# One transformer-block kernel: search bits in one set, per-unit score waits, and flags, sine arguments and new rows in pieces

## What is computed

```python
def _dsa_sparse_attention(q, k, v, q_idx, k_idx, w_idx):
    ...
        logits = jnp.einsum('bqhd,bsd->bqhs', qib, k_idx).astype(jnp.float32)
        score = jnp.einsum('bqhs,bqh->bqs', jax.nn.relu(logits), wb)
        limit = (tp // CHUNK + 1) * CHUNK
        admissible = key_pos[None, :] < limit[:, None]
        score = jnp.where(admissible[None], score, -jnp.inf)
        _, sel = lax.top_k(score, topk)
    ...
def _hybrid_layer(x, mem, cos, sin, ...):
    h = _rmsnorm(x, g_in)
    proj = h @ w_in
    ...
    y_a = _sliding_window_sink_attention(a_q, a_k, a_v, attn_sinks)
    y_b = _dsa_sparse_attention(b_q, b_k, b_v, b_qi, b_ki, b_wi)
    y_c = _memory_cross_attention(c_q, m_k, m_v)
    ys = jnp.stack([y_a * jax.nn.silu(a_z), y_b * jax.nn.silu(b_z), y_c * jax.nn.silu(c_z)], axis=2)
    u = jnp.einsum('bsnc,ncd->bsnd', ys, w_branch)
    merged = jnp.sum(jax.nn.sigmoid(gates) * u, axis=2)
    return x + merged @ w_out
```

## Time and profile before

| | |
|---|---|
| median of 3 runs | 3076.94 us (3074.46 to 3077.45) |
| the profiled execution | 3070.94 us, span 3069.2 us |
| busy: TensorE, VectorE, ScalarE, GpSimd | 2618.7, 1831.2, 1340.2, 474.3 us |
| mean granted TensorE clock | 0.931 of full speed |

### The profile page before, as it was taken

The page is one execution under the profiler, slowest core; times in us unless marked ns, Lnnn a source line. Parts: engine busy times, 40 slices in busy tenths (PEclk is TensorE's granted clock), DMA queues, the critical chain, the costliest instruction groups (busy, mean ns, idle before and its releaser), DMA issues.

```text
span 3069.2 us, 36940 instructions
## 1 busy us (share of the span) xinstructions
PE 2618.7 (85%) x13093; PEld 2163.2 (70%) x13093; DVE 1831.2 (60%) x3925; ACT 1340.2 (44%) x2550; POOL 474.3 (15%) x367
## 2 busy tenths in 40 slices
PE   4797988989888999998878898889888788877996
PEld 4575876867777778776667677777666566766785
DVE  3367665442677777315777767731588796666622
ACT  3354543332655444214656434431475672433511
POOL 3424243442010010101010010010101001000010
PEclk8898999989999999998989999999998889989998
DMA  3546564675443421454242421145424224001044
GB/s 120 196 159 201 163 213 144 214 258 186 151 148 105 145 98 63 169 198 155 92 142 97 130 90 42 42 164 196 155 86 134 83 96 137 28 21 34 30 165 158
DMA packets 172343, 399.33 MB, mean 130 GB/s; under 512 B 13568, under 2 KB 96512, under 8 KB 162176
## 3 DMA queue, kind: packets, MB, share of 16 engines
q1 hardware_dynamic: 172160, 396.96, 39.2%
HBM read 308.31 MB, written 88.60 MB: 129 GB/s over the span
## 4 chain that ended last, share of the span: by engine, by line
PE 46%; DVE 21%; ACT 14%; issue 12%; POOL 3%; DMA 3%; SPq 1%; DVEq 0%; ACTq 0%; POOLq 0%
PE PJ L760 31%; PE TR L661 5%; PE PV L727 5%; ACT signs L923 4%; DVE above L1353 2%; ACT ptH L912 2%; DVE ptL L1272 2%; ACT prob L899 2%; DVE prob L1233 2%; ACT prob L889 2%; DVE nmx L1243 2%; PE SC L670 1%; PE SC L671 1%; ACT squared L868 1%; DVE flags L1420 1%
## 5 line engine op out<-in xcount | busy, mean ns | idle before, releaser
L760 PE MATMUL PJ<-hH,pairs 128*128 128x512 f32 (+1 forms) x3584 | 1174.7, 398 | 56.9 <-POOL pairs L1055 18.3
L760 PEld LDWEIGHTS PJ<-hH,pairs 128*128 128x128 f32 x3584 | 690.1, 194 | 206.9 <-issue 37.6
L760 PE MATMUL PJ<-hL,pairs 128*128 128x512 f32 (+2 forms) x1792 | 711.8, 397 | 0.0
L923 ACT ACTIVATE signs<-score,bits 128x384 int8<-128x384 f32 (+7 forms) x256 | 335.7, 1311 | 275.2 <-DVE bits L1367 266.7
L1272 DVE TENSOR_TENSOR ptL<-TR,ptH 128x512 fp32r<-128x512 f32 (+1 forms) x384 | 257.1, 670 | 270.5 <-ACT ptH L912 268.9
L760 PEld LDWEIGHTS PJ<-hL,pairs 128*128 128x128 f32 (+1 forms) x1792 | 349.6, 195 | 66.3
L912 ACT ACTIVATE ptH<-TR 128x512 fp32r<-128x512 f32 (+1 forms) x384 | 221.2, 576 | 379.7 <-PE TR L661 378.8
L1353 DVE TENSOR_SCALAR_CACHE_REDUCE above<-score,bits 128x256 uint8<-128x256 f32 (+10 forms) x280 | 348.1, 1243 | 9.9
L760 PE MATMUL PJ<-ysH,pairs 128*128 128x512 f32 x768 | 271.7, 415 | 59.7 <-ACT sg L947 54.1
L661 PE MATMUL TR<-identR,prob 128*128 128x128 f32 x1480 | 235.7, 282 | 73.9 <-ACT prob L889 49.3
L661 PEld LDWEIGHTS TR<-identR,prob 128*128 128x128 f32 x1480 | 185.5, 144 | 140.1 <-ACT prob L889 66.2
(11 more groups left out here) (204 smaller groups left out, 3880.6 us busy)
## 6 DMA issues: line engine op xcount, KB each, us to landing
pairs<-w_split SPq DMA_DIRECT2D x444, 512.0 KB, 3.5
w_split<-pairs SPq DMA_DIRECT2D x74, 1024.0 KB, 4.9
raw<-in_w_in SPq DMA_DIRECT2D x106, 256.0 KB, 5.6
xs<-in_x SPq DMA_DIRECT2D x4, 2048.0 KB, 9.7
rows<-in_x SPq DMA_DIRECT2D x4, 2048.0 KB, 8.0
out<-rows SPq DMA_DIRECT2D x4, 2048.0 KB, 7.5
table<-trig SPq DMA_DIRECT2D x48, 128.0 KB, 3.5
raw<-in_w_branch SPq DMA_DIRECT2D x24, 256.0 KB, 5.8
```

The source lines that it names most:

```text
L760: done = nc.tensor.matmul(PJ[(st.u + half * up) % 2][0:min(st.width, P), 0:st.n_tok], lhs, rhs[:, row, 0:st.n_tok], start=(n % 12 == 0 and ...
L923: nc.scalar.activation(signs[:, 0:keys], score[:, tt, 0:keys], ACT.Sign, bias=thr.bitcast(F32)[:, tt:tt + 1], scale=-1.0, accum_out=cnt[:, ...
```

## The change

It has six parts. The search settles each bit for all four tiles in one set of operations, at the start of the next bit. One of the 32 bits stands ahead of the memory query units, and none behind the last unit of the sliding branch. The scores of attention A and B wait for the low part of their own query unit (`it.k`) and no longer for that of the last. "select" is cut: `exact` comes behind the first gate unit, and the six phases come two by two with branch B's first three query units. "prepare" is cut: SP loads the rows at the start of branch B's merge, ScalarE makes the squares after up unit m = 4, root and scaling follow gate unit m = 6. `tables` is a generator, of which a piece is made at each of the memory key and value units, and "sines" comes behind those.

```diff
-                if counting is not None:
+                if counting is not None and n_unit < len(specs):
                     select_bits(counting, PER_TURN)
+                if selecting is not None:
+                    for phase in range(2 * n_unit - 2, 2 * n_unit) if n_unit < len(specs) else range(2 * n_unit - 2, 6):
+                        steps.append(Step("select", g=selecting, i=phase))
+                if tables:
+                    steps.append(Step("tables", i=3 + n_unit))
...
     def prepare(source, g):
         steps.append(Step("prepare", source=source, g=g, used=n["pv"]))
+        if not g:
+            steps.append(Step("squares", source=source, g=g))
+            steps.append(Step("scale", source=source, g=g))
...
+            it.k = n["k"] - (3 - h) if branch != "c" else None
...
     for h in range(4):
         unit("mk", "w_mem_kv", h * P, n_tok=MEM, h=h)
+        steps.append(Step("tables", i=h))
     mem_keys = count["dve_pj"]
+    turned([("mv", "w_mem_kv", BW + h * P, dict(n_tok=MEM, h=h)) for h in range(4)], tables=True)
     steps.append(Step("sines"))
-    turned([("mv", "w_mem_kv", BW + h * P, dict(n_tok=MEM, h=h)) for h in range(4)])
...
+        select_bits(g, 1)
         for i in range(4):
             queries = unit("cq", "w_in", C_Q + i * P, i=i)
...
-        for role, src, col, more in z_b[:2]:
+        for place, (role, src, col, more) in enumerate(z_b[:2]):
             unit(role, src, col, **more)
-        select_bits(g, SEARCHED)
-        steps.append(Step("select", g=g))
-        turned([("q", "w_in", B_Q + i * P, dict(g=g, i=i)) for i in range(4)], beside=z_b[2:])
+            if place == 0:
+                select_bits(g, SEARCHED)
+                steps.append(Step("exact", g=g))
+        turned([("q", "w_in", B_Q + i * P, dict(g=g, i=i)) for i in range(4)], beside=z_b[2:], selecting=g)
         attention("b", g, branch_units(0, g, 2, 12), 24, 0)
         split_y()
+        if g + 1 < NG:
+            prepare("x", g + 1)
         for st in branch_units(1, g, 0, 12):
             steps.append(st)
+            if st.role == "gate" and st.m == 6 and g + 1 < NG:
+                steps.append(Step("scale", source="x", g=g + 1))
...
-            if st.m == 2 and g + 1 < NG:
-                prepare("x", g + 1)
+            if st.m == 4 and g + 1 < NG:
+                steps.append(Step("squares", source="x", g=g + 1))
...
             def scores(it, branch, g, chunks=None):
+                if branch != "c":
+                    pe.wait_ge(S["stack_lo"], it.k)
...
-                        pe.wait_ge(S["stack_lo"], st.k)
...
-            def settled(tiles, bit):
-
+            def settled(g, bit):
+
+
+                dve.wait_ge(S["signed"], 64 * g + 2 * (32 - bit))
+                link(TT(gi, cnt, limit, ALU.is_le))
                 if bit == 31:
-                    link(TS(found[:, tiles], gi[:, tiles], -1, None, ALU.add))
+                    link(TS(found, gi, -1, None, ALU.add))
                 else:
-                    link(STT(found[:, tiles], gi[:, tiles], bit, found[:, tiles], ALU.logical_shift_left, ALU.bitwise_xor))
...
                 for done in bits_done:
                     bit = 31 - done
-                    if done == 0:
-                        for t in range(2, NT):
-                            link(nc.vector.memset(limit[:, t:t + 1], admissible(g, t) - 2 * TOPK + 0.5))
+                    if done:
+                        settled(g, bit + 1)
+                        tried = TS(thr, found, 1 << bit, None, ALU.bitwise_xor)
                     else:
-                        signed(g, bit + 1)
-                    tried(slice(2, NT), bit).then_inc(S["thr_ready"], 1)
-                    link(tried(slice(0, 2), bit))
+                        for t in range(NT):
+                            link(nc.vector.memset(limit[:, t:t + 1], admissible(g, t) - (TOPK if t < 2 else 2 * TOPK) + 0.5))
+                        tried = nc.vector.memset(thr, 0)
+                    tried.then_inc(S["thr_ready"], 1)
+                    dve.wait_ge(S["thr_ready"], 32 * g + done + 1)
                     for t in range(2):
-                        count(g, t, ALU.is_ge)
-                    link(TS(gi[:, 0:2], cnt[:, 0:2], TOPK - 0.5, None, ALU.is_ge))
-                    settled(slice(0, 2), bit)
+                        count(g, t, ALU.is_lt)
```

37 lines of the change are left out of this document (18 added, 19 removed).

## The result

| | before | after |
|---|---|---|
| median | 3077.16 us (4 runs, 3074.46 to 3077.45) | 2990.53 us (4 runs, 2984.77 to 2993.31) |
| ratio, 95% interval | | 0.9718, 0.9701 to 0.9735 |
| profiled execution, its span | 3070.94, 3069.2 us | 2989.61, 2987.8 us |
| mean granted TensorE clock | 0.931 | 0.947 |

The change takes 86.6 us off the median. The forecast was 2993, with 84 us off.

A forecast was written before the change was run, and what follows sets the result against it. No engine is full; in-order TensorE waiting on chains through other engines bounds the kernel. Terms 29 + 21 + 20 + 14 = 84 us off give 2987 profiled, 2993 median; own range 2975 to 3010, with rivals 2962 to 3028.

The forecast's parts named there:

- (1): Search bits settled in one set: some 51 us of VectorE's small operations removed, 0 of it counted as gain.
- (2, 3): Sliding-attention heads: moved bit and scores waiting for their own query unit cut TensorE's 34.5 us of waits; gain 29 us.
- (4): Sparse branch's query units: threshold and selection spread in pieces instead of one VectorE block; gain 21 us, ends 14 and 31.
- (5): Third branch's units: rows loaded, squared and scaled apart, so three TensorE waits go; gain 20 us, ends 14 and 25.
- (6): Kernel start: sine arguments in pieces, so VectorE empties the first memory-key unit earlier; gain 14 us, ends 8 and 17.
- Rival A: Removed small search operations count in groups 2 and 3: 25 of 51 us on the path, 2968; chance 0.10.
- VectorE's busy time: Sign that the forecast is right: VectorE's busy time over the kernel about 35 us lower.
- The sliding attention of group 3 as long as before: Sign that removed search operations do not count there; if they did, it would be 3 to 6 us shorter.
- E: Sparse query units: VectorE's scan holds off GpSimd's add, delaying halvings and masked scores; 6 us, 2999; chance 0.12.
- B: Groups 2 and 3: VectorE and ScalarE pace attention, so TensorE's early starts are given back; 30 us, 3023; chance 0.12.
- C: Stage heads: many added short waits pull TensorE's clock down, 1.3 us each; 3123 with 100 waits; chance 0.03.
- D: Whole kernel: nothing much changes, waits replaced one for one by others; 3077; chance 0.03.

The follow-up runs named there:

- the quarters: The changed kernel with the next rows' 2 MB load cut into four of 512 KB, one behind each of the merge's first four units: 2978.44 us, 0.9693.

## Why the prediction was right

The part of each term that the runs bear out, in us. "Traces" is the sum of the steps in the list of starts above, by place, so that whatever (1) gives stands in the other rows; "undone" is the run with that part alone undone (for (2, 3) both), less the changed kernel, each known to about 7.

```
part                    forecast   traces   undone
(1) bits in one set          0        -       8.6
(2, 3) heads                29       36      34.4
(4) pieces                  21       19      20.0
(5) rows                    20       16      19.1
(6) sine arguments          14       10.5    15.4
sum                         84       81      97.5
```

**(1) was a miss of a small size.** "I take 0 of the 51." On the kernel before that holds (0.9993). In the changed kernel 8.6 of the 49 us counted. I priced the part against the trace of before and added it to parts that change that trace; that they thinned the cover which the step names, ScalarE's passes, is my reading, and no run shows it. Rival A's 25 is not reached; in group 3's memory query units ScalarE's copy still comes every 5.90 us, against 5.89 before.

```profile
2199.49 0.58 ACT L956 ACTIVATE qst<-PJ 128x512 fp32r<-128x512 f32 x1
...
2205.39 0.57 ACT L956 ACTIVATE qst<-PJ 128x512 fp32r<-128x512 f32 x1
```

**(2, 3)** The mechanism was right, and the wait that is left in sum: 5.1 forecast, 5.9 measured. Its shares were not, and the sum fits partly by luck: 3.3 forecast for group 3 and 1.8 for the others together, 1.75 and 4.2 measured. The moved bit costs 2.57 in group 3 (2.4 forecast). The term was 5 us too small. Behind each removed wait the traces show more than its length: in group 2 the wait fell by 5.9 (8.42 to 2.51) and the head gained 8.3. I had counted the clock for two heads of four.

**(4)** 21 forecast, 20.0 and 19 measured. With the part alone undone groups 3 to 0 lose 6.7, 6.2, 1.9 and 3.3, against 6.5, 7, 4 and 3 forecast, so only group 1 is off by half. The list of starts, which mixes in the other parts, has 8.0, 8.0, −1.0 and 4.0. In group 1 the swap's 4.18 is gone and a wait of 3.66 for masked scores stands in its place. The sentence "VectorE coming late to the first masked scores" stood in the sum for group 2 and was left out for group 1, and that is the step that failed there.

**(5)** Groups 1 and 2 gave 7.6 and 10.1 by the traces, against 6.8 and 7.9 (6.54 and 7.62, 1.3 of clock each, less 1 for the weights). "So the three waits go" is false for group 0. Its releaser in the earlier trace rows is GpSimd's split of raw weights, which the norm does not touch: those weights had stood behind the rows' load. I read all three rows as one family. The early load moved that wait to another unit, and the quarters removed it. The sign that ScalarE no longer waits for the rows was seen: 30.9 us in three waits before, none after.

**(6)** 12.0 us at the first normalised product against "some 14", and 11.6 there with the part undone; the wait of 15.11 fell to 5.28 (5.2 forecast).

**VectorE's busy time** fell by 24.0 us, not 35. The small operations of the bits fell by their 51 (158.5 to 107.0, the sums of their lines). The pieces of selection and tables, now beside GpSimd, take 22 us longer than they did (all phases together 138.6 against 124.4, the sine arguments 17.7 against 9.4), and two 4-word operations at the head of the phases 7 more (L1369 and L1370, 8.6 against 1.3). The 35 leave 16 for all that, and the prediction does not say from what. "The sliding attention of group 3 as long as before" did not hold either: the starts of the two kernels stand 71.8 us apart at its head and 74.4 at its last product, so it is 2.6 us shorter, and group 2's is 2.0 shorter. With (1) undone they are 1.5 and 2.0 longer again. That is rival A's sign, at less than the 3 to 6 us that it asks for, and it places some 3 of (1)'s 8.6.

**The rivals.** A and E are told above. B, early starts given back, would show as differences shrinking in groups 2 and 3; they grow there. In group 1, which B did not name, some is given back: between its sliding and its sparse head the delays of the runs with (1), with (3), and with (2) and (3) undone all shrink, by 3.1, 5.3 and 1.5 us. What takes it up there stays open. C: the clock rose, from 0.931 to 0.947. D: no.

**The total** came within 2.5 us, which is closer than its parts were. Against the undone column the terms were too small by 13.5 together, 8.6 of it in (1) and 5.4 in (2, 3). But that column sums to 97.5 where all parts together gave 86.6. The 10.9 between them can be read as parts that are worth more beside the others, so that undoing any of them loses the same microseconds; 6.5 of it would then lie in (1), worth 2 on the kernel before and 8.6 on the changed one. The runs do not show this. The changed kernel's own ratio is known to 0.0017, or 5 us, and enters the sum five times and the whole once, so that alone moves the gap by up to 20. A sum of parts, each priced on the trace of before, was right for the whole as far as these runs can tell. Whether two errors cancelled in it stays open. One slip is in the prediction's own range: 2975 to 3010 is not the ends of (4), (5) and (6) "taken half together" but taken whole (2993 less 18, and plus 19).

## What to carry to other kernels

Find the engine that waits at each head and read which single instruction is last: waiting for one's own operand and pulling one block of work out of that queue gave 34 of 87 us with nothing saved. A part priced at zero against a trace with waits should be priced again against the kernel without them: here it measured 2 us on the one and 8.6 on the other, if with too wide an error to be sure. And waits with different releasers are different waits, even at the same line: one of three "norm" waits was for weights queued behind the rows' load, and moving the load moved it along.

## What the runs showed of the hardware

A GpSimd add of 1.28 us took 4.59 beside a VectorE scan of 4.12, and VectorE's 4-word integer operation took 1.20 beside the add, and 0.16 alone in the kernel with the phases behind the halving. Short VectorE operations that I had counted as free pay a multiple of their length when they meet GpSimd: the six 512-column steps of the sine arguments took 0.69 each in one go, and 0.69 to 2.85 when spread beside weight splits. VectorE's rotations, which read PSUM, stayed at 0.68 beside GpSimd's splits (L1231 at 2490.88, beside L1081).

A transfer of 2 MB ahead of two of 256 KB in the same queue, with a store of 1 MB between them, made those land 11.4 and 11.9 us after issue rather than 5.6 to 5.9; with pieces of 512 KB, one ahead of each pair, they landed within 6.3.
